# Sample attention moved into the prompt attention's head-pair steps of a decoder trunk

## What is computed

```python
z = einsum('bqhd,bkhd->bhqk', q, k) * scale + bias
mask = k_pos < q_pos
log_1mb = where(mask, log_sigmoid(-z), 0.0)
after = cumsum(log_1mb, axis=3, reverse=True) - log_1mb
w = where(mask, exp(log_sigmoid(z) + after), 0.0)
o = einsum('bhqk,bkhd->bqhd', w, v)
y = (o * silu(gate)) @ w_out
```

## Time and profile before

| | us |
|---|---|
| median of 3 runs | 1160.44 (1160.05 to 1162.42) |
| the profiled execution | 1161.06 |
| its span, first to last instruction | 1159.3 |
| layer 0 and everything before layer 1's pair steps | 0 to 538 |
| pair steps 0 to 7 | 538 to 809.3 |
| pair steps 8 and 9 | 809.3 to 837 |
| the stage of the sample tokens | 837 to 1027.5 |
| `w_out_b` | 1027.5 to 1084 |
| embedding, final norm, stores | 1084 to 1159.3 |

### The profile page before, as it was taken

How to read it: one execution, slowest core, us unless ns; L and a number is a source line. 1 busy time by engine, 2 the same in 40 slices (tenths; PEclk the granted TensorE clock), 3 DMA queues, 4 the chain that set the end, 5 groups by cost and what they waited for, 6 DMA issues and landing times.

```text
span 1159.3 us, 20936 instructions
## 1 busy us (share of the span) xinstructions
PE 1089.7 (94%) x7896; PEld 988.3 (85%) x7896; DVE 630.8 (54%) x798; ACT 438.0 (38%) x654; POOL 400.4 (35%) x260
## 2 busy tenths in 40 slices
PE   4899979999999989999799999999689999999996
PEld 4799969999999989999798888898366776679996
DVE  6645545553345546655567656656446565436634
ACT  4111135442133332423344555654543544312421
POOL 6152056632255514346331122100025453604331
PEclk8999989999999989999899999999779999989998
DMA  8322202233322242322232222131427566432201
GB/s 224 109 70 76 72 25 84 72 90 101 91 56 74 70 128 73 91 73 59 70 92 74 84 81 83 50 103 29 143 73 252 183 217 217 129 89 76 73 1 77
DMA packets 152867, 111.17 MB, mean 96 GB/s; under 512 B 4482, under 2 KB 138770, under 8 KB 152722
## 3 DMA queue, kind: packets, MB, share of 16 engines
q1 hardware_dynamic: 152818, 110.49, 31.7%
HBM read 103.53 MB, written 6.95 MB: 95 GB/s over the span
## 4 chain that ended last, share of the span: by engine, by line
PE 89%; DVE 6%; ACT 2%; issue 1%; POOL 1%; DMA 0%; DVEq 0%; ACTq 0%; POOLq 0%
PE acc L1187 61%; PE ob L1469 4%; PE acc L1453 3%; PE zb L1506 2%; PE zb L1370 2%; PE ob L1506 2%; PE ob L1397 2%; PE ob L1386 2%; PE zb L1515 1%; PE acc L1351 1%; PE zb L1318 1%; DVE vt L1715 1%; PE zb L1489 1%; PE acc L1586 1%; PE zb L1477 1%
## 5 line engine op out<-in xcount | busy, mean ns | idle before, releaser
L1187 PE MATMUL acc<-act_hi,w_hi 128*128 128x272 f32 x1904 | 406.5, 295 | 18.2 <-DVE w_lo L1603 7.6
L1187 PE MATMUL acc<-act_hi,w_lo 128*128 128x272 f32 x1904 | 396.8, 290 | 0.0
L1187 PE MATMUL acc<-act_lo,w_hi 128*128 128x272 f32 x1904 | 396.2, 290 | 0.0
L1187 PEld LDWEIGHTS acc<-act_hi,w_hi 128*128 128x128 f32 x1904 | 301.9, 191 | 24.1 <-issue 9.9
L1187 PEld LDWEIGHTS acc<-act_lo,w_hi 128*128 128x128 f32 x1904 | 302.9, 191 | 0.0
L1187 PEld LDWEIGHTS acc<-act_hi,w_lo 128*128 128x128 f32 x1904 | 300.8, 191 | 0.0
L689 POOL TENSOR_TENSOR raw<-raw,cols 128x1024 f32<-128x1024 f32 x80 | 164.6, 2067 | 229.9 <-DMA raw<-in_w_in_b_dram 95.7
L1603 DVE TENSOR_TENSOR w_lo<-raw,w_hi 128x1024 fp32r<-128x1024 f32 x120 | 179.8, 1499 | 36.1 <-ACT w_hi L870 35.1
L870 ACT ACTIVATE w_hi<-raw 128x1024 fp32r<-128x1024 f32 x120 | 126.9, 1060 | 187.2 <-PE acc L1187 129.9
L839 POOL TENSOR_TENSOR vp_lo<-vpage,vp_hi 128x2048 fp32r<-128x2048 f32 x16 | 72.8, 4553 | 62.0 <-ACT vp_hi L1135 62.0
L1864 DVE TENSOR_TENSOR_SCAN left<-rest,zeros 128x512 f32<-128x512 f32 (+3 forms) x64 | 54.2, 847 | 47.0 <-ACT rest L1025 47.0
(11 more groups left out here) (264 smaller groups left out, 1393.9 us busy)
## 6 DMA issues: line engine op xcount, KB each, us to landing
raw<-in_w_in_a_dram SPq DMA_DIRECT2D x48, 512.0 KB, 3.9
kpage<-in_cache_k_dram SPq DMA_DIRECT2D x32, 512.0 KB, 4.8
vpage<-in_cache_v_dram SPq DMA_DIRECT2D x64, 256.0 KB, 3.2
raw<-in_w_out_a_dram SPq DMA_DIRECT2D x16, 512.0 KB, 3.9
raw<-in_w_ple_gate_dram SPq DMA_DIRECT2D x16, 512.0 KB, 3.9
raw<-in_w_kv_dram SPq DMA_DIRECT2D x16, 512.0 KB, 4.1
raw<-in_w_in_b_dram SPq DMA_DIRECT2D x16, 512.0 KB, 4.2
raw<-in_w_out_b_dram SPq DMA_DIRECT2D x8, 512.0 KB, 4.2
```

The source lines that it names most:

```text
L1187: mm = pe.matmul(t[:, c, 0:TH], wt[:, s, kt, :], xt[:, kt, c * TH:(c + 1) * TH], start=start and kt == kts[0] and wt is w_hi and xt is xh, ...
```

## The change

The stage of the sample tokens is gone. Each pair step does the sample attention of its pair, for all eight batches together, in plain float32 (no hi and lo parts), with the sigmoid form that the prompt uses in place of the softplus form.

- **Keys.** In step i SP loads, for each batch, the 128 columns of pair i from its four pages (64 KB a transfer), into a ring of four. PE turns batch b's four tiles into a bank of its own in slot n = b (`turn_keys`), ACT copies them into `kp_t` (`keep_keys`).
- **Logits.** In slot 0 of the next step `logits_sample` multiplies them with the queries, which POOL has laid out per batch (`queries`). Batch b is on output partitions 32*(b%4) to 32*(b%4)+31, so four products have four different groups of 32 columns of the array; batches b and b+4 add into one group, with zeros in the other's query columns. The 32 new keys go into `zb[1]` in the same way.
- **Weights.** ACT makes four sigmoids (512, 32, 512, 32 columns), DVE scans and multiplies 544 columns (slot 1), PE turns 4+1 tiles (slot 2), ACT copies them.
- **Values.** `values_sample` runs for batches 0 to 3 in slot 4 and 4 to 7 in slot 7, into the free columns of `ob[0]`; SP loads V as it does K. DVE copies the 256 columns in the next step, PE turns them (slot 4), DVE picks each batch's 4 columns and multiplies by the silu.
- **Dense products half by half.** A panel's slot now works half of the tokens over the whole contraction, each half in one bank out of three in turn, and DVE reads each half by itself; the fourth bank of `acc` is the key bank. K and V of the pair are turned into `zb` (slots 4 and 6).
- **Around it.** The splits of the attention's output into hi and lo parts move out of the steps into steps 8 and 9 (`split_o`, three pairs at a time). `turn_p` moves between the fourth and the fifth `w_out_b` panel. SP reads all 32 page numbers once, ahead of the pair steps.

The diff, cut to its core:

```diff
 @@ sync
+            page = [[sp.value_load(pages[0:1, b * PAGES + g:b * PAGES + g + 1], min_val=0, max_val=NPOOL - 1)
+                     for g in range(PAGES)] for b in range(NB)]
+            def load_keys(i, b):
+                if not isinstance(i, int) or i * NB + b >= RING:
+                    wait_apart(sp, k_turned, i * NB + (b - RING + 1))
                 for g in range(PAGES):
+                    src = ck_v[bass.ds(page[b][g], 1), :, cols_of(i)].rearrange("a t d -> t (a d)")
+                    sp.dma_start(kpage[:, b % RING, g, :], src).then_inc(k_in[b % RING], 16)
+            def load_values(i, r, js):
+                if not isinstance(i, int) or i * 2 + r > 0:
+                    wait_apart(sp, v_used, i * 2 + r)
...
+            def step(i, b, first=False):
+                if not first:
+                    load_values(i - 1, 0, range(2, 4))
+                load_keys(i, 4)
+                load_keys(i, 5)
+                load_panel(i + 1, 3)
+                load_keys(i, 6)
+                load_keys(i, 7)
+                load_panel(i + 2, 0)
+                if not first:
+                    load_values(i - 1, 1, range(4))
+                last = isinstance(i, int) and i == NP - 1
+                if not last:
+                    load_keys(i + 1, 0)
+                load_panel(i + 2, 1)
+                if not last:
+                    load_keys(i + 1, 1)
+                    load_keys(i + 1, 2)
+                store_pair(i, b)
+                load_panel(i + 2, 2)
+                if not last:
+                    load_keys(i + 1, 3)
+                load_values(i, 0, range(0, 2))
 @@ scalar, pair_step
+                    if att and n == 0:
+                        betas_sample(i - 1)
...
+                    if att and n == 2:
+                        keep_weights_sample()
+                    if dense:
+                        for b in (key_turns_0 if first else key_turns)[n]:
+                            keep_keys(b)
 @@ tensor
+            def half_products(t, s, c):
+                for kt in range(KT):
+                    for wt, xt in ((w_hi, act_hi[1]), (w_hi, act_lo[1]), (w_lo, act_hi[1])):
+                        mm = pe.matmul(t[:, 0:TH], wt[:, s, kt, :], xt[:, kt, c * TH:(c + 1) * TH],
+                                       start=kt == 0 and wt is w_hi and xt is act_hi[1],
+                                       stop=kt == KT - 1 and wt is w_lo)
 logits:
+                if k == 1:
+                    pe.wait_ge(betas_s, pair_s.now())
+                if k == 2:
+                    pe.wait_ge(ws_made, pair_s.now())
...
+            def turn_keys(b):
+                pe.wait_ge(k_in[b % RING], keys.lap(NB) * (32 * PAGES) + (b // RING + 1) * 16 * PAGES)
+                if keys.reg is not None or keys.now() > 0:
+                    pe.wait_ge(k_copied, keys.now())
+                keys.step()
+                for g in range(PAGES):
+                    mm = pe.transpose(key_bank[:, g * P:(g + 1) * P], kpage[:, b % RING, g, :], ident[:, :])
+                mm.then_inc(k_turned, 1)
+            def logits_sample(par):
+                pair_s.step()
+                pe.wait_ge(betas_made, blk.now() * 2)
+                pe.wait_ge(qz_set, pair_s.now() * 4)
+                pe.wait_ge(k_copied, pair_s.now() * NB)
+                for r in range(2):
+                    for j in range(RING):
+                        pe.matmul(zb[0][j * NS:(j + 1) * NS, :], qz[:, r * RING + j, :], kp_t[:, r * RING + j, :],
+                                  start=r == 0, stop=r == 1, skip_group_check=True)
+                for r in range(2):
+                    for j in range(RING):
+                        pe.matmul(zb[1][j * NS:(j + 1) * NS, 0:NS], qz[:, r * RING + j, :], kts[:, par, :],
+                                  start=r == 0, stop=False, skip_group_check=True)
+                pe.matmul(zb[1][:, 0:NS], row_of[:, :, :], unseen_n[:, :, :], start=False, stop=True,
+                          skip_group_check=True).then_inc(zs_full, 1)
+            def values_sample(r, par):
+                if r == 0:
+                    pe.wait_ge(ws_made, pair_s.now())
+                    pe.wait_ge(o_read, opair.now(1))
+                    pe.matmul(ob[0][:, 0:2 * P].rearrange("p (r d) -> p r d", r=2), wn_t[:, :],
+                              vs_nat[:, par, :][:, None, :].to_broadcast([NS, 2, P]), start=True, stop=False,
+                              skip_group_check=True)
+                for j in range(RING):
+                    pe.wait_ge(v_in[j], pair_s.now(-1) * (32 * PAGES) + (r + 1) * 16 * PAGES)
+                for g in range(PAGES):
+                    for j in range(RING):
+                        rows_j = slice(j * NS, (j + 1) * NS)
+                        mm = pe.matmul(ob[0][rows_j, r * P:(r + 1) * P], wp_t[:, g, rows_j], vpage[:, j, g, :],
+                                       start=False, stop=g == PAGES - 1, skip_group_check=True)
+                mm.then_inc(v_used, 1)
 pair_step, slot n:
+                            mm = half_products(take_third(), s, n % 2)
...
+                    if att and n == 0:
+                        logits_sample(1 - par)
                     if att and n >= 2:
                         turn_weights((n - 2) // 2, n % 2)
+                    if att and n == 2:
+                        turn_weights_sample()
+                    if att and n == 4:
+                        values_sample(0, 1 - par)
+                    if prev and n == 4:
+                        turn_outputs()
+                    if att and n == 7:
+                        values_sample(1, 1 - par)
+                    if dense and n == 4:
+                        turn_natural(kt_t[:, par, :])
+                    if dense and n == 6:
+                        turn_natural(vt_t[:, :])
+                    if dense:
+                        if first and n == 2:
+                            pe.wait_ge(acc_read, ACC_B + 2)
+                        for b in (key_turns_0 if first else key_turns)[n]:
+                            turn_keys(b)
 @@ w_out_b
+                if n == SLOTS - 1:
+                    turn_p(1)
```

More of the change, by code:

```diff
@@ L302, in build @@
[L302 to L309, removed]
+        kts = place("kts", [P, 2, NS], F32, at)
+        qts = place("qts", [P, NS], F32, at)
+        silu_s = place("silu_s", [P, 2, NS], F32, at)
@@ new lines, in _ @@
+            sp.wait_ge(out_done, 16)
+            nc.disable_value_cache = True
+            for b in range(RING):
+                load_keys(0, b)
+            for k in range(4):
+                load_panel(0, k)
+            for k in range(3):
+                load_panel(1, k)
+            step(0, 0, True)
+            step(1, 1)
+            with repeat(sp, NP // 2 - 2, (panel, 8)) as m:
+                step(m * 2 + 2, 0)
+                step(m * 2 + 3, 1)
+            step(NP - 2, 0)
+            step(NP - 1, 1)
@@ L1150, in _ @@
[L1150 to L1165 removed]
+            split_o(NP - 1, 1)
@@ L1166, in _ @@
+            for n in range(KT):
+                split_x(n, 1, gain=g_ple_c[1])
+                split_next()
+                if n == SLOTS - 1:
+                    split_p(1)
             embed(1)
@@ L1401, in pair_step, with turn_outputs @@
+            def turn_outputs():
+                olds.step()
+                pe.wait_ge(o_kept, olds.now())
+                pe.wait_ge(betas_made, blk.now() * 2)
+                for r in range(2):
+                    mm = pe.transpose(zb[1][:, (r + 1) * P:(r + 2) * P], o_rows[:, r, :], ident[:, :])
+                mm.then_inc(os_turned, 1)
             def pair_step(par, dense, att, prev, first=False):
@@ L1556, in _ @@
-            mm.then_inc(os_full, 1)
-            turn_logits()
-            keys(range(KT // 2))
-            step_s(False)
-            with repeat(pe, NB - 3, (accs, TURNS_B), (kseq, 1), (lseq, 1), (seq, 1)):
-                step_s()
-            step_s(True, True, False)
-            step_s(True, False, False)
-            turn_outputs()
-            turn_p(1)
-            for n in range(KT):
-                if n == 0:
-                    gemm_by_halves(0, o_lo, NP + 1)
-                else:
-                    gemm(0)
+            for n in range(KT):
+                pe.wait_ge(lo_made, panel.now(1))
+                t = take_acc()
+                for kt in range(KT):
+                    if n == 0:
+                        pe.wait_ge(o_lo, kt + 1)
+                    mm = products(t, panel.slot(SLOTS), act_hi[0], act_lo[0], [kt], kt == 0, kt == KT - 1)
+                mm.then_inc(panel_done, 1)
+                panel.step()
+                if n == SLOTS - 1:
+                    turn_p(1)
@@ L1923, in pair_step @@
[L1923 to L1928 removed]
+                        turned_pair(k_nat, ks_nat, par)
+                    if dense and n == 7:
+                        turned_pair(vb_nat, vs_nat, par)
```

873 lines of the change are left out of this document (338 added, 535 removed).

## The result

The changed kernel takes 1093.66 us (median of 4 runs, 1091.87 to 1095.97); the kernel before takes 1160.75 in the runs beside it. The ratio is 0.9423, with a 95% interval of [0.9407, 0.9439]: 67 us less. The forecast was 1081, some 13 us too low, with the time inside its range. The profiled execution took 1095.97 us, the longest of the four; its span is 1094.2 us.

The account below looks back on a forecast made before the run. TensorE, busy 94% of the span, was taken as the bound. From 538: 42.4 + 42.3 + 6 x 45.5 + 48 + 60.5 + 75.3 = 541.5, a span of 1079.5, so 1081 us; range 1054 to 1135.

Parts of the forecast that it names:

- What is removed, and TensorE's price: 190.5 us of sample stage go; the sample work adds 9.4 us of TensorE time to a 34.1 us pair step.
- fours for the tiles: Sample products on four 32-column tiles run side by side, at 0.42 ns a column; the rival, only twos, 1112 us, chance 0.09.
- The price of a column: A plain float32 product on TensorE costs 1.69 ns a column, from 0.91 us for two ones-matrix products of 272 columns.
- SP as cover: SP's 72 issues a step at 0.6 us, 43 us, stay hidden under the 45.5 us step, but barely.
- its bound of 0.64: Cost c of a page transfer, in us, at which SP, needing 64c + 4.8 a step, takes over.
- SP becomes the bound: Rival: page issues on SP set the step; c = 0.72 gives about 1120 us; chance 0.13 for 0.64 to 0.80, 0.05 above.
- Both of the signs: SP never waiting in a step means it is the bound; `k_in` or `v_in` waits in steady steps mean the forecast is wrong.
- The wait in slot 0: TensorE waits 2.0 us in each step, before the sample logits, for ScalarE's sigmoids that free `zb`.
- The clock: TensorE's granted clock stays at 1.00 in steps 2 to 7.
- The rival priced 2.5 a step: Wait and turns drop TensorE's clock to half in each step: 2.5 us a step in 7 steps, 1099 us; chance 0.09.
- Steps 8 and 9: Last two steps, a chain through three engines often at half clock, with a late V load: 48 us.
- step 0: First pair step: TensorE stops after three halves, the rest follows the norm's wait; 42.4 us in place of 35.4.

Follow-up runs that it names:

- all edits: Whole computation with SyncE's and TensorE's loops written out, last V early, silu as sigmoid times gate on GpSimd, against the changed kernel: 1051.89 us, 42 less.

## Why the prediction was right, and where it was 13 us off

- **What is removed, and TensorE's price.** Right. 34.1 + 9.4 = 43.5 us was the forecast of TensorE's work in a step; steps with nothing late take 43.35 (260.1 for six). The four turns of one batch take 0.44 us, as 16 in 1.75 before. Taking fours for the tiles was right too: the two calls of sample values take 2.0 us and the logits 1.9, for 1.7 each in the sum. (The price of a column was slightly misread: 0.91/544 is 1.67 ns and not 1.69, and four turns take 0.66 us in the earlier trace rows and not 0.6; neither moves a step by more than 0.2 us.) The Trainium skill's 2.38x (TensorE: Matmul & The Clock Gate, Part 3) is for three column tiles; four reach 3.5 here, by the estimate above.
- **SP as cover: the step that failed.** 64 issues at 0.6 us plus 4.8 were to hide under 45.5. The pitch of the loop, from start to start, was well judged (0.62), but 64 of it, 39.7 us, leave 12.7 of a step's 52.4 for the other eight issues, the long ones and the loop itself, where the sum had 4.8. It had nothing for long issues (eleven in the 164 us of the chain, some 9 us above the usual 0.33) nor for the 2.44 us at the jump. By the prediction's own form, 64c + 4.8 = 52.4 gives c = 0.74, above its bound of 0.64. So the rival "SP becomes the bound" came true, in part: it was priced for 7.5 steps and held in three, those that SyncE's loop feeds. Written out, the pitch is 0.52. Both of the signs that the prediction named for this came: SyncE waits for nothing in steps 3 to 5, and TensorE waits there for V, 2.9, 5.9 and 2.6 us.
- **The wait in slot 0.** Right in cause and size: 2.0 forecast, 2.2 to 2.3 measured (1.0 in step 5), for the sigmoids behind the table loads of the earlier trace rows. Wrong in place: it shows in four of steps 2 to 7, not in the ones where TensorE came late for another reason. That it goes from these steps with the table loads is shown.
- **The clock.** The forecast had 1.00 in steps 2 to 7. Idle time of 2 to 6 us brings it to its lower level at times: busy time in the six steps is 271.3 us, 11 above the 260.1 of steps without idle time. The rival priced 2.5 a step; it is about 1.9, and it goes when the waits go. The same 2.26 us brought it down behind some waits and not behind others; what decides that stays open.
- **Not seen: the stop of TensorE's loop,** 3.8 and 3.0 us. The loop of before has none (six steps of 34.1), with two thirds of the instructions.
- **Steps 8 and 9.** 8.8 us too long a forecast. The wait for V is real (5.10 us), but the sample values came 20 us after the start and not 26.8, since more of the chain ran at full clock: `values` took 2.30 us there. That the whole came out only 13 us off is in part luck: these 8.8 us, and 2.1 of step 0, hid part of the 24 by which steps 2 to 7 were forecast too short.
- **Together:** the six steps take 297.2 us, 37.1 above TensorE's own 260.1: 25.9 of idle time and 11.2 of half clock. With SyncE's loop written out 14.8 and 8.1 remain (four waits of 2.2, two stops of 2.9); with all edits, none.

## What to carry to other kernels

Cost the issuing queue like an engine, with its address arithmetic and its slow issues, once the sum leaves it a cover as thin as here (43 us under 45.5); an address in a register inside a loop, with the loop's own jump, turned the cover into the bound. When several late things end close to each other, undoing one may show nothing, or less than it is worth: take them away together before a cause is ruled out. A wait also costs the half clock behind it, here 0.4 us for each us of idle time in the changed kernel (11.2 for 25.9) and 0.8 with SyncE's loop and the table loads gone (5.4 for 6.4).

## What the runs showed that I had not expected

- A loop of TensorE over two steps (some 1700 recorded instructions) stops 2.2 to 3.8 us at its jump back; the loop of before, with 1100, doesn't stop. SyncE's loop stops 2.44 us at its own. Both are "issue" in the chain, with no releaser.
- SyncE's arithmetic ahead of an issue takes 0.14 us with page and columns both in registers, 0.05 with the columns constant; single issues of the same 64 KB take up to 1.7 us for the usual 0.33.
- Products on four 32-column tiles overlap 3.5 times in turn, and 1.5 times with eight records of a tile in a row.
